# The feed-forward of a fused transformer kernel: the first weight, too, by seven half-size products

## The reference

```python
D_FF = 4 * D_MODEL

def rmsnorm_2(x, g):
    xf = x.astype(jnp.float32)
    y = xf * lax.rsqrt(jnp.mean(xf * xf, axis=-1, keepdims=True) + EPS)
    return (y * g.astype(jnp.float32)).astype(x.dtype)

def squared_relu_mlp(n, w_up, w_down):
    return jnp.square(jax.nn.relu(n @ w_up)) @ w_down
```

## Time and profile before

| | before |
|---|---|
| median of 3 runs | 1579.47 us (1578.11 to 1579.8) |
| the profiled execution | 1579.45 us |
| its span, first to last instruction | 1577.6 us |
| TensorE busy | 1559.4 us, 99% |
| VectorE busy | 1036.2 us, 66% |
| ScalarE busy | 726.6 us, 46% |
| GpSimd busy | 680.8 us, 43% |
| granted TensorE clock | 0.999 of full speed |

### The profile page before, as it was taken

One profiled execution on the slowest core, in us unless ns is written; L12 is line 12 of the kernel. 1 busy time (PEld: TensorE's weight loads), 2 busy tenths in 40 slices (PEclk: granted clock), 3 DMA queues, 4 the chain that ended last, 5 costly groups with the idle time before them and its releaser, 6 DMA issues.

```text
span 1577.6 us, 20552 instructions
## 1 busy us (share of the span) xinstructions
PE 1559.4 (99%) x7570; PEld 1279.8 (81%) x7570; DVE 1036.2 (66%) x1343; ACT 726.6 (46%) x1085; POOL 680.8 (43%) x666
## 2 busy tenths in 40 slices
PE   9999999999999999999999999989999999999999
PEld 8888787787778898788888888778886888888887
DVE  7434554675688977558484857877777557574847
ACT  6323433325245665345353535566765453444433
POOL 0002110104345453286665748442333574857574
PEclk9999999999999999999999999999999999999999
DMA  7232222232211211422323131222121414141321
GB/s 246 80 107 80 80 80 80 96 107 80 95 66 54 85 63 54 160 81 102 112 81 134 57 135 50 81 80 81 54 81 33 155 54 160 54 159 55 137 77 54
DMA packets 25731, 145.07 MB, mean 92 GB/s; under 512 B 3936, under 2 KB 5680, under 8 KB 9264
## 3 DMA queue, kind: packets, MB, share of 16 engines
q1 hardware_dynamic: 25648, 143.95, 26.4%
HBM read 141.84 MB, written 2.10 MB: 91 GB/s over the span
## 4 chain that ended last, share of the span: by engine, by line
PE 85%; DVE 11%; ACT 3%; issue 1%; POOL 1%; DVEq 0%; ACTq 0%; POOLq 0%
PE ps_G L613 19%; PE ps_G L614 19%; PE ps_G L615 19%; PE ps_C L1247 5%; PE ps_C L1248 5%; PE ps_C L1246 5%; DVE wide L2626 1%; DVE top L2622 1%; PE ps_AV L1076 1%; PE ps_C L699 1%; PE ps_AV L1247 1%; PE ps_AV L1246 1%; PE ps_AV L1248 1%; PE ps_AV L825 1%; PE ps_C L798 1%
## 5 line engine op out<-in xcount | busy, mean ns | idle before, releaser
L613 PE MATMUL ps_G<-ch,wh 128*128 128x512 f32 x800 | 319.9, 400 | 2.5 <-DVE wl L2221 1.8
L615 PE MATMUL ps_G<-ch,wl 128*128 128x512 f32 x800 | 312.1, 390 | 0.0
L614 PE MATMUL ps_G<-cl,wh 128*128 128x512 f32 x800 | 312.0, 390 | 0.0
L613 PE MATMUL ps_G<-nh,wh 128*128 128x512 f32 x504 | 199.7, 396 | 0.4 <-DVE h L2494 0.2
L2935 DVE TENSOR_TENSOR wl<-raw,wh 128x1024 fp32r<-128x1024 f32 (+1 forms) x104 | 179.1, 1740 | 31.0 <-ACT wh L1885 25.2
L615 PE MATMUL ps_G<-nh,wl 128*128 128x512 f32 x504 | 196.3, 390 | 0.0
L614 PE MATMUL ps_G<-nl,wh 128*128 128x512 f32 x504 | 196.2, 389 | 0.0
L613 PEld LDWEIGHTS ps_G<-ch,wh 128*128 128x128 f32 x800 | 150.6, 188 | 42.1 <-issue 7.6
L614 PEld LDWEIGHTS ps_G<-cl,wh 128*128 128x128 f32 x800 | 150.6, 188 | 33.5 <-issue 3.4
L615 PEld LDWEIGHTS ps_G<-ch,wl 128*128 128x128 f32 x800 | 150.5, 188 | 31.7
L2221 DVE TENSOR_TENSOR wl<-raw,wh 128x2048 fp32r<-128x2048 f32 x46 | 108.3, 2354 | 62.3 <-ACT wh L1388 59.2
(11 more groups left out here) (429 smaller groups left out, 3184.2 us busy)
## 6 DMA issues: line engine op xcount, KB each, us to landing
raw<-wst SPq DMA_DIRECT2D x96, 1024.0 KB, 4.9
raw<-quart_d SPq DMA_DIRECT2D x16, 1024.0 KB, 4.8
tabs<-quart_d SPq DMA_DIRECT2D x8, 1024.0 KB, 7.1
mixed_buffers<-quart_d SPq DMA_DIRECT2D x8, 1024.0 KB, 4.9
raw<-wst SPq DMA_DIRECT2D x8, 256.0 KB, 6.2
out<-wide SPq DMA_DIRECT2D x8, 256.0 KB, 2.0
h<-xT SPq DMA_DIRECT2D x7, 256.0 KB, 6.3
raw<-wst SPq DMA_DIRECT2D x2, 512.0 KB, 5.3
```

The source lines that it names most:

```text
L613: mm(o, ah, bh, start=first, stop=False)
L614: mm(o, ah, bl, start=False, stop=False)
L615: return mm(o, al, bh, start=False, stop=last)
```

## The change

The up phase is now done by seven half-size products too. A part has 14 products, numbered k = 0 to 13: 0 to 6 up, 7 to 13 down.

- `up_product` takes 4 chunks by 4 output blocks by three matmuls of 256 columns (half of the tokens), 48 matmuls; there are 336 in a part. The outputs go to UX = (G0, G1), UY = (C0, C1), UV = (C2, AV), and quadrants of the result are kept in `wide`: ScalarE copies a finished pair out (`keep`), VectorE adds a later one to it (`join`).
- h is no longer multiplied by the normalisation's factor r before the first weight. Since relu(r x) squared is r squared times relu(x) squared, each token's r squared is applied in `add_up`, which turns from an addition into a multiply-add with a factor for each token. The token sums come from four matmuls of one column each (`token_stat`).
- Three of the four quadrants of the hidden values are squared by VectorE (`squared`, 2 instructions each), the fourth by ScalarE.
- All 14 weights of a part are split in halves by `weight_half`. Eight of them are sums of quadrants. Four of these GpSimd adds (s3, s1, t3, t1), four are made by transfers that GpSimd starts and that add an SBUF buffer onto another (s2, s4, t2, t4): ten loads of 1 MB in a part where there were eight, and five adding transfers (s2 in two halves). The six weight buffers change roles from part to part (`buffer`).
- The activation operands of the up products are made once for each layer by GpSimd, ScalarE and VectorE (`enter`, `feed_up`, `low_up`, `operand`).
- The accumulators start from h in both layers: `turn_h` runs in the first one as well, and the final addition of h turns into a copy.

The diff's core, without the bookkeeping of buffers and of the last part:

```diff
+UX, UY, UV = ("G0", "G1"), ("C0", "C1"), ("C2", "AV")
...
+DOWN = UP
...
+    ROLE = ("a11", "a12", "s2", "s3", "s1", "a22", "a12", "b11", "b21", "t2", "t3", "t1", "b21", "b22")
...
+            def down_loads(pt):
+                f, p, n = pt.f, pt.p, pt.g + 1
+                split_done(pt, 0)
+                sp.wait_ge(weight_sums, 8 * n - 6)
+                load_weight(pt, "t1", quart_d[f, p, B12])
+                split_done(pt, 2)
+                sp.wait_ge(s4_in, 16 * n)
+                load_weight(pt, "b22", quart_d[f, p, B22])
+                split_done(pt, 3)
+                sp.wait_ge(s2_first, 16 * n)
+                sp.wait_ge(s2_second, 16 * n)
+                load_weight(pt, "b11", quart_d[f, p, B11])
+                split_done(pt, 5)
+                load_weight(pt, "t2", quart_d[f, p, B11])
+                split_done(pt, 6)
+                load_weight(pt, "b21", quart_d[f, p, B21])
...
+            def next_up_loads(pt):
+                nx, n = Part(pt.f, pt.p + 1), pt.g + 1
+                f, p = nx.f, nx.p
+                split_done(pt, 7)
+                sp.wait_ge(weight_sums, 8 * n)
+                load_weight(nx, "s1", upq_d[f, p, A21])
+                split_done(pt, 9)
+                sp.wait_ge(t4_in, 16 * n)
+                load_weight(nx, "a22", upq_d[f, p, A22])
+                split_done(pt, 10)
+                sp.wait_ge(t2_in, 16 * n)
+                load_weight(nx, "a11", upq_d[f, p, A11])
+                split_done(pt, 12)
+                load_weight(nx, "s2", upq_d[f, p, A22])
+                split_done(pt, 13)
+                load_weight(nx, "a12", upq_d[f, p, A12])
             def layer_loads(f):
...
-            def up_block(pt, k, each=None):
...
-                for c in range(KC):
...
-                    ins = three(o[:], wh[s][:, c, col:col + P], wl[s][:, c, col:col + P], mh[:, c, :], ml[:, c, :],
-                                c == 0, c == KC - 1)
...
+            def up_product(pt, k, banks, fresh, x, need=lambda c: None, between=lambda c: None):
+                s = pt.slot(k)
+                ah, al = product_weight(wh[s]), product_weight(wl[s])
+                xh, xl = x
+                for c in range(4):
+                    if c % 2 == 0:
+                        pe.wait_ge(half_lo, pt.half(k, c // 2))
+                    need(c)
+                    for b in range(4):
+                        o, w = ps[banks[b // 2]][:, b % 2 * TW:(b % 2 + 1) * TW], slice(b * P, (b + 1) * P)
+                        mm(o, ah[:, c, w], xh[:, c, :], start=fresh and c == 0 and b % 2 == 0, stop=False,
+                           skip_group_check=True)
+                        mm(o, ah[:, c, w], xl[:, c, :], start=False, stop=False, skip_group_check=True)
+                        ins = mm(o, al[:, c, w], xh[:, c, :], start=False, stop=c == 3, skip_group_check=True)
+                    if c % 2:
+                        ins.then_inc(half_done, 1)
+                    between(c)
...
+                    pe.wait_ge(kept, 8 * g + 2)
+                    operand(1)
+                    up_product(pt, 2, UX, False, XT2, between=token_sums)
+                    if pt.first:
+                        pe.wait_ge(acc_from_h, 8 * f + 8)
+                    else:
+                        pe.wait_ge(acc_added, pt.adds)
+                    operand(2)
+                    up_product(pt, 3, UY, True, XT3)
+                    pe.wait_ge(kept, 8 * g + 4)
+                    operand(3)
+                    up_product(pt, 4, UX, False, XT1)
+                    pe.wait_ge(kept, 8 * g + 6)
+                    operand(4)
+                    up_product(pt, 5, UY, False, XT4)
+                    pe.wait_ge(joined, 6 * g + 4)
+                    up_product(pt, 6, UX, False, X22)
...
+            def weight_half(pt, k, a):
+                role, n, x = Part.ROLE[k], pt.g + 1, slice(1024 * a, 1024 * (a + 1))
+                if k == 2:
+                    act.wait_ge((s2_first, s2_second)[a], 16 * n)
+                elif k in (3, 4, 10, 11):
+                    act.wait_ge(weight_sums, 8 * pt.g + {3: 0, 4: 2, 10: 4, 11: 6}[k] + a + 1)
+                elif k in (6, 9, 12):
+                    act.wait_ge({6: s4_in, 9: t2_in, 12: t4_in}[k], 16 * n)
+                else:
+                    act.wait_ge(buffer_in[pt.buffer(role)], 16 * pt.loads(role))
+                if k > 1 or not pt.first:
+                    act.wait_ge(half_done, pt.half(k - 2, a))
+                A(flat(wh[pt.slot(k)])[:, x], weights_of(pt, role)[:, x], ACT.Copy).then_inc(half_hi, 1)
...
+                    for n in range(2):
+                        A(quadrant(0, 1, n), ps[UX[n]][:].rearrange("p (c n) -> p c n", c=2), ACT.Relu).then_inc(kept, 1)
+                    for n in range(2):
+                        q = quadrant(0, 1, n)
+                        act.wait_ge(kept, 8 * g + 7 + n)
+                        A(q, q, ACT.Square).then_inc(hid_twice, 1)
+                        act.wait_ge(hid_twice, 2 * g + n + 1)
+                        A(ring_hi[:, 1, 2 * n:2 * n + 2, :], q, ACT.Copy).then_inc(row_hi, 1)
...
+            def weight_sum(dst, x, y, parts=range(8)):
+                for n in parts:
+                    w = slice(n * TW, (n + 1) * TW)
+                    ins = g.tensor_tensor(dst[:, w], x[:, w], y[:, w], ALU.add)
+                    if n % 4 == 3:
+                        ins.then_inc(weight_sums, 1)
...
+                for a, sem_ in enumerate((s2_first, s2_second)):
+                    pool.wait_ge(weight_sums, 8 * n - 7 + a)
+                    w = slice(1024 * a, 1024 * (a + 1))
+                    g.dma_start(s2[:, w], s3[:, w], accum_op=ALU.add).then_inc(sem_, 16)
...
+                    pool.wait_ge(half_lo, pt.half(1, 1))
+                    pool.wait_ge(s2_first, 16 * n)
+                    pool.wait_ge(s2_second, 16 * n)
+                    g.dma_start(s4, s2, accum_op=ALU.add).then_inc(s4_in, 16)
+                    weight_in(pt, "t1", "b22")
+                    pool.wait_ge(half_lo, pt.half(4, 1))
+                    weight_sum(t3, b22, t1_)
+                    weight_in(pt, "t2")
+                    pool.wait_ge(weight_sums, 8 * n - 2)
+                    g.dma_start(t2, t3, accum_op=ALU.add).then_inc(t2_in, 16)
+                    weight_in(pt, "b11")
+                    weight_sum(t1_, t1_, b11)
+                    pool.wait_ge(hid_set, 6 * pt.g + 6)
...
+                        value_sum(3 * c, s1[:, c, :], a22, a21, ALU.subtract)
+                        value_sum(3 * c + 1, a21, a21, a11, ALU.subtract)
+                        pool.wait_ge(value_sums, sums + 3 * c + 2)
+                        value_sum(3 * c + 2, a11, a11, s1[:, c, :], ALU.add)
+                    pool.wait_ge(half_lo, pt.half(8, 1))
+                    pool.wait_ge(t2_in, 16 * n)
+                    g.dma_start(t4, t2, accum_op=ALU.add).then_inc(t4_in, 16)
+                    pool.wait_ge(value_sums, sums + 12)
+                    for c in range(4):
+                        a11, _, a12, _ = halves(c)
+                        pool.wait_ge(row_lo, 3 * pt.g + c // 2 + 2)
+                        value_sum(12 + c, a12, a11, a12, ALU.subtract)
+                    if not pt.last:
+                        nx = Part(f, p + 1)
+                        weight_in(nx, "a11", "s1")
+                        pool.wait_ge(half_lo, pt.half(11, 1))
+                        weight_sum(weights_of(nx, "s3"), weights_of(nx, "a11"), weights_of(nx, "s1"))
+                        second_sum(nx)
+                        weight_in(nx, "a22")
+                        weight_sum(weights_of(nx, "s1"), weights_of(nx, "s1"), weights_of(nx, "a22"))
                 if not f:
...
+                    def join(k, at, banks, row, tokens):
+                        dve.wait_ge(kept, 8 * g + at)
+                        dve.wait_ge(half_done, pt.half(k, 1))
+                        for n in range(2):
+                            q = quadrant(row, tokens, n)
+                            tt(q, q, ps[banks[n]][:].rearrange("p (c n) -> p c n", c=2), ALU.add).then_inc(joined, 1)
+                    def squared(at, row, tokens, keep):
+                        for n in range(2):
+                            q = quadrant(row, tokens, n)
+                            dve.wait_ge(joined, 6 * g + at + n)
+                            stt(out=q, in0=q, scalar=0.0, in1=q, op0=keep, op1=ALU.mult).then_inc(hid_set, 1)
...
+                    lo(6, 0)
+                    join(4, 6, UX, 1, 1)
+                    lo(6, 1)
+                    squared(3, 1, 1, ALU.min)
+                    dve.wait_ge(row_hi, 3 * g + 1)
+                    subtract(ring_hi[:, 0, :, :], ring_lo[:, 0, :, :], quadrant(1, 1)).then_inc(row_lo, 1)
+                    lo(7, 0)
+                    join(5, 6, UY, 1, 0)
+                    lo(7, 1)
+                    squared(5, 1, 0, ALU.min)
+                    lo(8, 0)
```

(29 more changed lines are left out.)

751 lines of the change are left out of this document (423 added, 328 removed).

## The result

The changed kernel takes **1650.91 us** (median; 1649.6 to 1653.49) against 1579.63 us before (1578.11 to 1579.81): ratio 1.0455, 95% interval 1.0437 to 1.0474. It is slower by 71 us. The forecast was 1584 us with a range of 1562 to 1612, so it was wrong, on the slow side.

A forecast was written before the change was run, and what follows sets the result against it. TensorE, busy 99% of the span, was taken to bound the kernel. 1579.45 us, less 25.6 for matmuls, plus 3.5 for transposes, 2 for layer entry and 8 x 3.1 for stalls, gave 1584 us, range 1562 to 1612.

The forecast's parts named there:

- TensorE's own time: Up phase falls from 43.5 to 40.3 us a part, down phase unchanged; 25.6 us saved over eight parts.
- The step of 0.120 us: Time between starts of 256-column matmuls in the up phase, taken from the trace; 336 make 40.3 us a part.
- The stalls: TensorE waits in product 9: 1.4 us at its start, 1.7 at chunk 3; together 3.1 us a part.
- The twelve sums can start when the last squares end: GpSimd's activation sums before product 9 start at 42.1 us into the part and end at 56.9.
- The place: TensorE idles 20 to 30 us in all before product 9's first and fourth chunks, released by VectorE's second pair.
- The adding transfers: GpSimd-started transfers take 7.8 us each, land within 10 us, and cost nothing in the total.
- the ring: Rival: sums, transfers and loads, closing once a part, set the pace; 1615 us or 1647 us; chance 0.11.
- 0.47 + 0.40: Chances of stalls of 2.1 to 4.5 us a part (1576 to 1595 us) and below 2.1 (1559 to 1575).

The follow-up runs named there:

- z1: The changed kernel with each GpSimd sum, of weights and of activations, made over 8 of its 256 columns, all waits and starts kept: 1556.84 us.
- x2: The changed kernel with GpSimd waiting once, for the first sum behind each transfer start of t2, t4 and s2: 1615.42 us.
- y2: x2 with t1's eight GpSimd sums turned into an adding transfer, started behind t2's: 1590.87 us.
- y3: y2 with all squares made by ScalarE and VectorE's first pair put before half (9,1): 1578.90 us.
- z3: z1 with the adding transfers also made over 128 of their columns: 1555.23 us.
- v1: r1 with eight more GpSimd sums replacing s2's transfers in parts two to four of each half, and s1's sums behind s4's start: 1618.19 us.
- r1: x2 with SP loading a11 before a22: 1619.29 us.
- x3: The changed kernel with the starts of the t2, t4 and s2 transfers moved behind the sums, no added wait: 1639.67 us.

## Why the prediction was wrong

- *TensorE's own time: right.* Forecast without any stall: 1559.4 us, TensorE busy 1537. z1 shows 1556.84 and 1537.2. The step of 0.120 us holds in the changed kernel (891.79 to 894.79 is 25 steps). The Trainium skill's 109 ns for such a step (TensorE: Matmul & The Clock Gate, section "Back-to-back issue gap", where the formula is given for the gap of an isolated matmul) does not show here either.
- *The stalls: the step that failed.* Forecast s = 3.1 us a part, bounds 0 and 5, from VectorE's operations of 512 columns at 0.88 us, "up to 1.08". Measured against z1: 94.1 / 8 = 11.8 us a part. The term of the sum 8 x 3.1 = 24.8 us was in truth 94.1. Three things were missing.
  - The price of a 512-column operation beside GpSimd had its bound from one row, in a kernel where GpSimd started no transfer. The longest was 6.89 us. The holds and the waits that they made cost 35.5 us (x2). The trace before could not show it; the bound should have said that starts on this engine were new.
  - "The twelve sums can start when the last squares end", at 42.1. In x2, free of holds, the last squares end at 43.0 (887.98, the part starting at 844.95) and the sums start at 45.3, because t1's eight sums stand ahead of them on the same queue. I had priced GpSimd's sums (1.23 us; x2 shows (904.06 - 890.21) / 12 = 1.15) and forgotten whose turn it was. Moving that work off the engine (x2 to y2) gave 24.5 us back, by its turn and by its load together. The 34.0 us that y2 still loses against z1, 4.3 a part, compare with the 3.1 of the forecast; with ScalarE's squares and the early first pair (y3) 22.1 are left.
  - A stall was priced at its length. TensorE comes out of a wait of 3 us at the lower clock, and some 120 slow steps added about 25 us, which lie within the sums above: with shorter waits x2 has some 35 of them and y3 one or two.
- *The place: half right.* The second pair (L3306), its fourth chunk above all, releases 28.9 us of TensorE's idle time, where 20 to 30 us at product 9 were forecast. That the number fits is luck: about 3 us of it in each part stand behind the hold of t4's start. The wait ahead of product 7, for VectorE's join L3224, was not foreseen; it is 28.0 of the 57.1 us.
- *The adding transfers: right to cost at nothing, as far as tested.* By group medians they land 6.9 to 7.1 us after issue for s4 and t4, 10.5 to 11.8 for t2 (forecast 7.8, and within 10). Beside small sums their size changed nothing (z3), and whole sums in place of s2's changed nothing either (v1 against r1). When they start does matter: late (x3), it cost 24 us against x2. The rival that ended on the slow side near 1647 us (the ring) had nearly the right time by luck, for the wrong reason.
- *The chance.* 0.47 + 0.40 stood on a stall below 4.5 us. VectorE was busy for 85% of the down half before anything was added; that should have widened the range upwards.

## What to carry to other kernels

When a change adds work to an engine that shares something with a busy one, write out that engine's queue in order and give every item a start time, not only a price. Behind each transfer that GpSimd starts, look whether dense work of its own follows; one semaphore wait behind the first piece is a cheap test. A stall of TensorE is to be priced with the slow steps that follow it, and the saving itself is checked by one run in which the suspected work is made small and all waits are kept.

## What the runs showed of the hardware

- The hold: where GpSimd's sums stand right behind a transfer's start, a VectorE instruction with two inputs in SBUF that begins in the start or in the run lasts until the run ends: 3.5 us behind t4's start, 5.1 to 5.4 behind s2's, 5.9 to 7.1 behind t2's. GpSimd's sums then take 0.73 us each. An operation on PSUM inside such a run takes 0.73 us (851.79, L3240), as elsewhere. With one wait in the run both engines share: x2's squares take 0.7 to 2.1 us and a sum 1.35.
- The Trainium skill (SBUF — State Buffer, section "SBUF: two separate sides") says that VectorE and GpSimd share a port pair which the one that starts first keeps for the whole instruction. The ordinary rows agree: 1.76 us for a half that takes 1.14 alone is one sum (0.70) more, at most. The hold does not: by the rule the square would wait for one sum, 1.4 us in all, and it waited for eight. It had even begun before the first of them (887.2 against 887.66, so in seven of the eight parts), in the time of the start. Why the start ahead of the run matters is open; that the wait removes it is shown.
- Of two adding transfers of 1 MB started together (y3: t2's and t1's) the first lands after 8.1 to 11.8 us and the second after 12.4 to 16.1. Not started in pairs they took 6.9 to 12.2 in the changed kernel.
- TensorE's clock fell behind the waits of 3.16 us; y3, with waits of up to 0.9 us in the third part, has one or two slow steps in all. No run took the length of a wait as its one variable.
